# Gates of the prompt heads multiplied in the last projection, and combined token blocks of the second input stage fetched in halves

## The reference

```
h = RMSNorm(x);  z = h @ W_in
y = [branch(z) * silu(gate), memattn(z) * silu(mgate)] @ W_out
x = x + y
```

## Time and profile before

| | |
|---|---|
| median of 3 runs | 2329.01 us (2326.93 to 2332.37) |
| profiled execution | 2325.68 us, span 2324.0 us, mean granted clock 0.975 |
| PE busy / DVE / ACT / POOL | 2191.2 / 1292.5 / 1008.1 / 434.2 us |
| projection of layer 0 ends, input stage begins | about 794 to 802 us |
| attention stage | about 1500 to 2126 us |
| last projection | 2127 us to the end |
| PE's wait for the samples' values at the start of the attention stage (L3077) | 1.74 us, until 1510.00 |
| ACT: rounding of half a block, 1056 columns (L317) / of y, 2048 columns (L1999) | 1.07 / 1.92 us |
| DVE: remainder of a weight row of the projection, 1024 columns (L2048) | 1.23 us |
| layer 0's boundary: DVE takes tile 7's x (L2059) | 787.16 us |

### The profile page before, as it was taken

The page is one execution under the profiler, slowest core; times in us unless marked ns, Lnnn a source line. Parts: engine busy times, 40 slices in busy tenths (PEclk is TensorE's granted clock), DMA queues, the critical chain, the costliest instruction groups (busy, mean ns, idle before and its releaser), DMA issues. The chain is left out here.

```text
span 2324.0 us, 47107 instructions
## 1 busy us (share of the span) xinstructions
PE 2191.2 (94%) x18709; PEld 1824.9 (79%) x18709; DVE 1292.5 (56%) x2040; ACT 1008.1 (43%) x2090; POOL 434.2 (19%) x542
## 2 busy tenths in 40 slices
PE   7799999988999689999999997889999999998999
PEld 7799899876688589999999997666666656654787
DVE  6846667535423454334444442688888888774211
ACT  7534223224311244333333343457777777775100
POOL 0533223102000132222222220311121111100000
PEclk9899999998999889999999999989999999999999
DMA  8232222153635733334533336779999999978331
GB/s 292 85 97 79 81 65 69 62 201 133 223 114 147 219 128 99 111 102 129 159 111 93 103 102 250 249 288 397 397 404 396 405 394 390 378 280 301 117 109 55
DMA packets 283274, 453.98 MB, mean 195 GB/s; under 512 B 30962, under 2 KB 208062, under 8 KB 283038
## 3 DMA queue, kind: packets, MB, share of 16 engines
q1 hardware_dynamic: 274958, 421.83, 52.1%
q0 software_dynamic: 8000, 29.10, 3.3%
q10 hardware_dynamic: 96, 0.02, 0.0%
HBM read 372.43 MB, written 78.43 MB: 194 GB/s over the span
## 5 line engine op out<-in xcount | busy, mean ns | idle before, releaser
L365 PE MATMUL h_bank<-h_t_hi,h_w 128*128 128x264 f32 x1568 | 453.8, 289 | 25.3 <-DVE h_t_lo L322 17.3
L367 PE MATMUL h_bank<-h_t_hi,h_w 128*128 128x264 f32 x1568 | 447.9, 286 | 0.0
L366 PE MATMUL h_bank<-h_t_lo,h_w 128*128 128x264 f32 x1568 | 447.6, 285 | 0.0
L365 PEld LDWEIGHTS h_bank<-h_t_hi,h_w 128*128 128x128 f32 x1568 | 297.8, 190 | 26.6 <-issue 22.6
L367 PEld LDWEIGHTS h_bank<-h_t_hi,h_w 128*128 128x128 f32 x1568 | 298.0, 190 | 0.0
L366 PEld LDWEIGHTS h_bank<-h_t_lo,h_w 128*128 128x128 f32 x1568 | 298.0, 190 | 0.0
L365 PE MATMUL p_bank<-h_t_hi,h_w_hi 128*128 128x264 f32 x896 | 257.5, 287 | 13.0 <-DVE h_t_lo L322 10.4
L367 PE MATMUL p_bank<-h_t_hi,h_w_lo 128*128 128x264 f32 x896 | 255.3, 285 | 0.0
L366 PE MATMUL p_bank<-h_t_lo,h_w_hi 128*128 128x264 f32 x896 | 255.0, 285 | 0.0
L276 DVE TENSOR_TENSOR h_w<-l_w,h_w 128x512 fp32r<-128x512 f32 x164 | 127.4, 777 | 164.6 <-ACT h_w L269 163.3
L365 PEld LDWEIGHTS p_bank<-h_t_hi,h_w_hi 128*128 128x128 f32 x896 | 169.5, 189 | 14.1 <-issue 12.9
(11 more groups left out here) (372 smaller groups left out, 4749.5 us busy)
## 6 DMA issues: line engine op xcount, KB each, us to landing
ar_arena<-in_cache_sb_k_dram SPq DMA_DIRECT2D x73, 768.0 KB, 9.7
bf_vpage<-in_cache_sb_v_dram SPq DMA_DIRECT2D x64, 768.0 KB, 9.0
b_vpage<-in_cache_sb_v_dram SPq DMA_DIRECT2D x64, 768.0 KB, 8.5
l_w<-in_w_in_sb_dram SPq DMA_DIRECT2D x55, 512.0 KB, 4.6
l_w<-in_cache_sb_k_dram SPq DMA_DIRECT2D x36, 768.0 KB, 10.0
l_w<-in_w_in_pool_dram SPq DMA_DIRECT2D x32, 512.0 KB, 4.2
bf_kpage<-in_cache_sb_k_dram SPq DMA_DIRECT2D x19, 768.0 KB, 9.0
ar_arena<-scratch_yT SPq DMA_DIRECT2D x14, 1024.0 KB, 6.6
```

Source lines behind the costliest of these rows:

```text
L365: pe.matmul(out, w_hi, t_hi, start=kk == 0 and x in ("P1", "P2", "P5"), stop=False, skip_group_check=True)
L366: pe.matmul(out, w_hi, t_lo, start=False, stop=False, skip_group_check=True)
L367: ins = pe.matmul(out, w_lo, t_hi, start=False, stop=kk == K2 - 1, skip_group_check=True)
```

## The change

Two parts, in one program.

1. *Gates.* In the attention stage only the first 128 tokens of each head are multiplied by their gates (`g0`, 64 KB per head). The other tokens' output is copied to `yh` and stored without the gates. The last projection fetches for each tile t from 1 on the gates of its 128 tokens (12 x 128 x 128, 768 KB) behind y, into the place of y_lo, and DVE multiplies them into y (`gate`) before ACT rounds it. For t = 1 that stands between the remainders of weight rows 11 and 12.
2. *Halves.* Token blocks 2 to 6 of the input stage get places that are free before the projection of layer 0 has ended, and are fetched in halves of 264 columns: the first half, which needs the tokens up to tile 6 only, in the last iteration of that projection, the second in the input stage after the stores of tile 7 (`tok_stored`). The first pair's second weight tile gets a place of its own (`wb0`) and is fetched there too. POOL makes the weight sum for P5 and the next one, ACT and DVE round it and the first halves of blocks 5 and 4, and PE does the first half of P5, all in the projection's block. Blocks 2, 3 and 6 are rounded whole as before, when both halves are there. The projection's block no longer waits for the last stores of the token blocks.

```diff
@@ -87,6 +87,7 @@
 PLACES = 8
+EARLY_PLACES = (("t_lo", 2), ("t_lo", 3), ("t_lo", 6), ("t_lo", 4), ("t_hi", 4), ("t_lo", 5), ("t_hi", 5))
@@ -111,7 +112,9 @@
             k.sem(n) for n in ("t_first", "t_second", "t_added", "t_high", "t_rest"))
-        self.fetched = [k.sem(f"fetched{n}") for n in range(8)] if i else None
+        self.fetched = [k.sem(f"fetched{n}") for n in range(7)] if i else None
+        self.fetched_first = {n: k.sem(f"fetched_first{n}") for n in (4, 5)} if i else None
+        self.tok_stored = k.sem("tok_stored") if i else None
@@ -163,11 +163,23 @@
         self.w_full, self.w_hi, self.w_lo = full[:, :, 1], rounded[:, :, 0], rounded[:, :, 1]
+        for n, (kind, t) in enumerate(EARLY_PLACES):
+            here = where - size * (n + 1)
+            if kind == "t_hi":
+                self.hi[t] = at(f"t_hi{t}", [P, K2, HALF], F32R, here)
+            else:
+                self.full[t] = at(f"t_lo{t}_full", [P, K2, HALF], F32, here)
+                self.lo[t] = at(f"t_lo{t}", [P, K2, HALF], F32R, here)
...
+        self.wb0 = at("wb0", [P, KD, P], F32, bottom + 4 * KD * P)
...
+
+    def wb_of(self, p):
+
+        return self.wb0[:, :, :] if self.i and p == 0 else self.wb[p % 2]
@@ -301,12 +313,15 @@
         sp.dma_start(self.full[t][:, :, cols], tok[t, :, :, cols].rearrange("k p t -> p k t")
-                     ).then_inc(self.fetched[7 if cols.start else t], 16)
+                     ).then_inc(self.fetched_first[t] if t in (4, 5) and cols.start == 0 else self.fetched[t], 16)
...
-            act.wait_ge(self.fetched[7 if cols.start else t], 16)
+            if t in (4, 5) and cols.start == 0:
+                act.wait_ge(self.fetched_first[t], 16)
+            else:
+                act.wait_ge(self.fetched[t], 32 if t in (2, 3, 6) else 16)
@@ -336,18 +351,18 @@
         for t, n in {0: ((0, 3), (1, 4)), 1: ((4, 5),), 2: ((2, 6),), 3: ((3, 7),), 4: ((6, 8),)}.get(i, ()):
-            self.token_rest(dve, t, n)
+            self.token_rest(dve, t, n + self.i, slice(SUB if self.i and t == 4 else 0, HALF))
...
-        rests = {"P1": 1, "P2": 2, "P5": 3} if self.i else {"P5": 1, "P1": 3, "P2": 4}
-        rests.update({"P6": 5, "P3": 6, "P7": 7, "P4": 8})
+        rests = ({"P1": (1, 1), "P2": (2, 2), "P5": (3, 5), "P6": (4, 6), "P3": (7, 7), "P7": (8, 8), "P4": (9, 9)} if self.i else
+                 {"P5": (1, 2), "P1": (3, 3), "P2": (4, 4), "P6": (5, 5), "P3": (6, 6), "P7": (7, 7), "P4": (8, 8)})
...
-                pe.wait_ge(self.t_rest, rests[x] + n * (x == "P5"))
+                pe.wait_ge(self.t_rest, rests[x][n])
@@ -1936,6 +1956,9 @@
                     sp.dma_start(y[:, :, :], yT[:, :, tok(t):tok(t) + P].rearrange("k p t -> p k t")).then_inc(s["yl"], 16)
+                    if i:
+                        sp.dma_start(gates[t % 2], S["gT"][:, :, tok(t):tok(t) + P].rearrange("k p t -> p k t")
+                                     ).then_inc(s["gatel"], 16)
@@ -1959,6 +1982,7 @@
                         q.load_a(sp, 0)
+                        q.load_b(sp, 0)
@@ -1971,8 +1995,14 @@
                             norm.load_other(sp, t)
+                    if norm and t == N - 1:
+                        sp.wait_ge(s["ready"], 2 * N)
+                        q.token_fetch(sp, S["tok"], 5, FIRST)
...
+                    if norm and t == N - 1:
+                        for n in (4, 2, 3, 6):
+                            q.token_fetch(sp, S["tok"], n, FIRST)
@@ -1984,7 +2014,7 @@
                     norm.store(sp, N - 1)
-                    sp.wait_ge(norm.stored, 16 * norm.stores(N + 1))
+                    q.tok_pieces = norm.stores(N + 1)
@@ -1992,7 +2022,10 @@
                 def part(t):
-                    act.wait_ge(s["yl"], 16 * (t + 1))
+                    if i and t:
+                        act.wait_ge(s["mixed"], t)
+                    else:
+                        act.wait_ge(s["yl"], 16 * (t + 1))
@@ -2029,9 +2062,18 @@
                             q.token_high(act, n)
+                if norm:
+                    q.token_high(act, 5, FIRST)
+                    q.round(act, 2)
+                    q.token_high(act, 4, FIRST)
...
+                def gate(t):
+                    dve.wait_ge(s["yl"], 16 * (t + 1))
+                    dve.wait_ge(s["gatel"], 16 * t)
+                    dve.tensor_tensor(y[:, 0:HEADS, :], y[:, 0:HEADS, :], gates[t % 2], ALU.mult).then_inc(s["mixed"], 1)
+
@@ -2040,6 +2082,8 @@
                         rest(0)
+                    if i and at == KM - 4:
+                        gate(1)
@@ -2060,6 +2104,8 @@
                         norm.normed_of(dve, t, x[:, t % 2, :])
+                    if i and t + 2 < N:
+                        gate(t + 2)
@@ -2075,6 +2121,18 @@
                             q.token_rest(dve, n, n + 1)
+                if norm:
+                    q.token_rest(dve, 5, 3, FIRST)
+                    q.remainder(dve, 2)
+                    q.token_rest(dve, 4, 4, FIRST)
+
+            @block.gpsimd
+            def _(gp):
+                if norm:
+                    gp.wait_ge(s["ready"], 2 * N)
+                    gp.wait_ge(norm.normed, norm.at[N - 2] + 1)
+                    gp.wait_ge(ol[0], 16 * (N // 2))
+                    q.combine(gp, 2)
@@ -2116,7 +2174,7 @@
                                 ins.then_inc(s["ready"], 1)
-                            if norm and (t, at, half) == (N - 1, SPLIT, 1):
+                            if norm and (t, at, half) == (N - 1, SPLIT + 1, 1):
@@ -2125,6 +2183,8 @@
                     q.product(pe, 1, range(1, 2))
+                    pe.wait_ge(s["added"], 2 * N)
+                    q.product(pe, 2, range(1))
@@ -2162,12 +2223,12 @@
                 memory.place("mp")
-                q.load_b(sp, 0)
-                for n in range(2):
-                    q.token_fetch(sp, S["tok"], 5, slice(n * SUB, (n + 1) * SUB))
+                sp.wait_ge(q.tok_stored, 16 * q.tok_pieces)
+                for t in (5, 4):
+                    q.token_fetch(sp, S["tok"], t, SECOND)
...
-                for t in (4, 2, 3, 6):
-                    q.token_fetch(sp, S["tok"], t)
+                for t in (2, 3, 6):
+                    q.token_fetch(sp, S["tok"], t, SECOND)
@@ -2205,7 +2266,7 @@
             def _(gp):
-                for j in range(q.ahead + 1):
+                for j in range(3, q.ahead + 1):
@@ -2227,9 +2288,7 @@
                     q.copy(act, p, "P5", place(p, 1, 1), ACT.Copy)
-                q.round(act, 2)
-                for n in range(2):
-                    q.token_high(act, 5, slice(n * SUB, (n + 1) * SUB))
+                q.token_high(act, 5, SECOND)
@@ -2266,9 +2325,7 @@
                     dve.tensor_copy(new[:, r % 2, :], aux[0][0:SAMPLES, 0:P]).then_inc(s["rowed"], 1)
-                q.remainder(dve, 2)
-                for n in range(2):
-                    q.token_rest(dve, 5, n + 3, slice(n * SUB, (n + 1) * SUB))
+                q.token_rest(dve, 5, 5, SECOND)
@@ -2313,7 +2370,7 @@
                 for i, (p, x) in list(enumerate(q.seq))[2:]:
-                    q.product(pe, i)
+                    q.product(pe, i, range(1, 2) if i == 2 else range(2))
@@ -2423,7 +2481,7 @@
                      ).then_inc(self.rest, 16)
-        sp.dma_start(self.gh[:, 0, :], S["gT"][0, :, 0:SEQ]).then_inc(self.rest, 16)
+        sp.dma_start(self.g0[:, 0, :], S["gT"][0, :, 0:P]).then_inc(self.rest, 16)
@@ -2638,8 +2696,8 @@
                     if h >= 2:
-                        gp.wait_ge(ys[h % 2], 16 * (h // 2))
-                    gp.dma_start(gh[:, h % 2, :], S["gT"][h, :, 0:SEQ]).then_inc(gl[h % 2], 16)
+                        gp.wait_ge(s["oev"], 2 * (h - 2) + 1)
+                    gp.dma_start(g0[:, h % 2, :], S["gT"][h, :, 0:P]).then_inc(gl[h % 2], 16)
@@ -2813,8 +2871,12 @@
                         dve.wait_ge(begun.rest, 32)
-                    cols = slice(ch * 512, (ch + 1) * 512)
-                    dve.tensor_tensor(gh[:, h % 2, cols], obank[:, :], gh[:, h % 2, cols], ALU.mult).then_inc(s["oev"], 1)
+                    if ch == 0 and h >= 2:
+                        dve.wait_ge(ys[h % 2], 16 * (h // 2))
+                    if ch == 0:
+                        dve.tensor_tensor(yh[:, h % 2, 0:P], obank[:, 0:P], g0[:, h % 2, :], ALU.mult)
+                    edge = P * (ch == 0)
+                    dve.tensor_copy(yh[:, h % 2, ch * 512 + edge:(ch + 1) * 512], obank[:, edge:512]).then_inc(s["oev"], 1)
```

More of the change, by code:

```diff
@@ L330, in tokens_scalar @@
         for t in {0: (0, 1), 1: (4,), 2: (2,), 3: (3,), 4: (6,)}.get(i, ()):
-            self.token_high(act, t)
+            self.token_high(act, t, slice(SUB if self.i and t == 4 else 0, HALF))
     def tokens_vector(self, dve, i):
@@ L1778, in __init__ @@
         self.gl, self.squared, self.mean, self.root, self.inv, self.normed, self.turned, self.hi, self.lo, self.summed, \
[L1779 to L1780 removed]
+            self.ol, self.rl, self.first = (k.sem(n) for n in (
```

(7 more changed lines are left out.)

34 lines of the change are left out of this document (16 added, 18 removed).

## The result

The changed kernel is slower than before: 2332.8 us against 2328.1 (medians of 20 runs each, 4.7 us apart). The ratio of the two sets of runs is 1.0024 with an interval of 1.0016 to 1.0033, so 5.6 us (3.7 to 7.7). Timed again it was 1.0014 (1.0001 to 1.0026), 3.3 us. I had forecast 3 us less.

A forecast was written before the change was run, and what follows sets the result against it. DVE, not PE, was taken to bound the first 28 us of the input stage, PE the rest. Boundary 6.9 plus attention 0.5 minus last projection 4.4 gave 3.0 us less: 2326.0 us, range 2317 to 2333.

The forecast's parts named there:

- The start of the chain: Layer boundary: block 5's second half lands at 807.8, ACT rounds it in 1.0, DVE starts at 808.8.
- The phase change: End of the projection phase, when the input stage's first fetch is issued: 804.5, with 1.5 us for the change itself.
- the half P5: PE's first half of P5, in the projection's tail: starts at 800.4 instead of 811.5 and takes 2.6 us.
- The length of the chain: DVE's work in the input stage up to the pair's P5: 28.2 us shrinks to 20.0, plus 0.9.
- the 0.7 us that I took off for overlap: End of DVE's chain: taken as 829, between 829.7 by full sum and 828.7 if ACT's rounding overlaps.
- The tail's shift: Projection's tail: weight block fetched ahead of blocks 0 and 1 makes DVE's block 1 and all behind it 1.6 us late.
- The 0.7 us for POOL beside DVE: Projection's tail: POOL's two sums run beside DVE's subtraction for tile 7, costing DVE 0.7 us.
- The last projection: Tile 1's gates and product make row 13 of the first tile 4.4 us later; steady tiles hide theirs.
- the upper bound: Last projection: 4.4 us and a stretch at half clock after PE's gaps, some 2 us more.
- The attention stage: Fewer gate bytes there give almost nothing: 0.5 us earlier, between 4 earlier and 2 later.
- rival 2: The attention stage is bound by its DMA: 14.0 us come off there, 16.5 less in all, 2312.5; chance 0.05.
- Rival 4: Boundary: PE's half P5 keeps the phase open, stores are late; gives 1, 3 us more in all, 2332; chance 0.14.

The follow-up runs named there:

- stores_first: The changed kernel with tile 7's stores ahead of the early halves of blocks 2, 3 and 6; 0.7 us (-3.5 to 4.9) against before.
- h_two: As h_inside, but nothing of blocks 2, 3 and 6 fetched early, both their halves in the input stage; 0.9 us (-2.1 to 3.7) against before.
- h_final: As h_best, but the next pair's first weight tile fetched behind block 2, ahead of blocks 3 and 6; -6.1 us (-9.5 to -2.6) against before.
- h_best: As h_two, but the first pair's second weight tile fetched behind blocks 0 and 1; -0.9 us (-4.4 to 2.3) against before.
- h_inside: Only the halves, ordered as stores_first, second halves of 5 and 4 fetched ahead of the phase change; -3.3 us (-7.0 to 0.5) against before.

## Why the prediction was wrong

- *The start of the chain, wrong by 3.6 us, is the step that failed.* I had the early halves "through at 800, and 1.3 MB of stores behind them by 804: no later than the phase change, but not by much". The phase change came as forecast (40.4 us behind tile 6's x, forecast 40.1), the half P5 too (34.9; forecast 36.0). But the first fetch came at 43.1, not 40.1, and the half then took 3.8 us to ACT's rounding, not 3.3. I had summed bytes at 333 GB/s from the first issue (2.7 MB from 789 would even be through at 797). That leaves out that a store's issue is itself held back while four fetches fill the queue (4.41 us for the last three), and that 4.4 us more pass from the end of the last issue to the fetch that waits for the stores. Before, 801.85 - 797.5 had the same length with little in the queue, though the phase change lies in it. DVE began at 48.0 instead of 44.4. stores_first took this away and got 2.0 of it back.
- *The length of the chain, wrong by 1.3 us, failed too.* I had let the wait for the weight tile go, since it would land near 816. It came 57.8 us behind tile 6's x, as 822.2 on my scale: ACT waited 3.17 us and DVE 1.00. The chain took 22.2 us, not 20.9. And the 0.7 us that I took off for overlap did not come. The three make 5.6 us; 5.4 of the 6.9 were missing. h_two and h_final showed that this was the larger lever: with the start mended and this wait left, and grown to 6.9 us, P5 gained nothing; with both mended, 6.3 us against before. That this is close to my 6.9 is chance: I had forecast it for a kernel that did neither.
- *The tail's shift* of 1.6 us for the weight tile was right in kind (1.1 to 3.8 us in all profiles of kernels that fetch it ahead of blocks 0 and 1, none in h_best). The 0.7 us for POOL beside DVE were not: DVE's remainder took 2.35 us (at 791.09), and POOL's sum 3.36 in place of 1.3. It was POOL that waited:

```profile
791.09 2.35 DVE L337 TENSOR_TENSOR h_t_lo<-h_t_lo_full,h_t_hi 128x2112 fp32r<-128x2112 f32 x1
```

```profile
791.23 3.36 POOL L247 TENSOR_TENSOR h_w_full<-h_wb 128x512 f32<-128x512 f32 x1 [208.81 <-PE h_bank L83]
```

- *The last projection* was right in mechanism and size: 4.4 forecast, 4.1, 3.1, 5.8, 4.0 and 5.8 in five profiles. Row 13 came 3.1 to 4.4 us late in all five; in the two with 5.8 PE then ran on at a mean granted clock of 0.65 and 0.62 for four microseconds, where the others had 1.00. It is the stretch at half clock that I had only in the upper bound. The windows behind row 13, of stores_first and then of the changed kernel:

```profile
2165.00:2169.00 4.00, 3.70 (x15) 1.94 (x16) 2.51 (x3) 0.00 (x0) 0.00 (x0) 0.65 0.01 4
```

```profile
2165.00:2169.00 4.00, 3.69 (x21) 2.46 (x22) 2.52 (x3) 0.00 (x0) 0.00 (x0) 1.00 0.02 4
```

  That nothing of it would be hidden was right too, and that the steady tiles would hide theirs: 4.5 of 8.4 us used (forecast 4.4).
- *The attention stage* gave next to nothing, as forecast, and rival 2 fell with it. Between 1495 and 2125 us the eight profiles with the gates' part shift by -2.4 to 1.2 us against the first profile of before (mean -0.1), the eight others by 0.1 to 1.8 (mean 0.9).
- *Sum.* With 1.5 for the boundary in place of 6.9 my sum would have been 2.4 us slower, within the interval of the second timing (0.2 to 6.1), below that of the first (3.7 to 7.7). Of the first, 1 to 5 us are not explained by the changed places, and their cause stays open. Rival 4 comes nearest in outcome and time (3 us more), but not in its reason: PE's half P5 did not hold the stores back, the early halves did.

## What to carry to other kernels

A transfer started early is not free because its data has a place: whatever stands behind it in the same queue is late by its length, and what stands there may be what the next stage really waits for. Sort a queue by when each piece is first needed (here 5, 4, the sum's weights, 2, the next pair's weights, 3, 6) before splitting anything: that order alone was worth 5 us of P5 between h_best and h_final, while the early fetch of three halves had held up the start of the chain by 3.2 us (h_inside against h_two). And work moved onto the one tile that has no slack costs all of its length (4.4 us forecast, 3.1 to 4.4 measured at row 13), where the same work in the steady tiles is hidden.
